# First norm of a two-layer diffusion trunk: scale weights loaded ahead of shift weights, and four query tiles taken from X times gain with the shift as a bias

## What is computed

```python
sh1, sc1, g1, sh2, sc2, g2 = silu(cond) @ ada_w[l] + ada_b[l]      # six vectors of 1024, for c_ctx and for c
h = rms_norm(x, norm1_g[l]) * (1.0 + sc1) + sh1
qa, fa_f, fa_b, ia, ga, qb, kb, vb, ob, gates = split_cols(h @ w_in, EVEN_SPLITS)
qa = silu(qa)                                                       # HGRN2 queries, 4 heads of 128
f  = lb + (1.0 - lb) * sigmoid(f_raw)                               # forget gates, per direction
```

## Time and profile before

| | us |
|---|---|
| median of three runs | 1123.31 |
| the profiled run, whole | 1123.68 |
| its span, first to last instruction | 1121.9 |
| PE busy | 1066.8 (95%) |
| DVE, ACT, POOL busy | 499.0, 412.2, 553.3 |
| mean granted PE clock | 0.981 |

### The profile page before, as it was taken

One profiled execution on the slowest core, in us unless ns is written; L12 is line 12 of the kernel. 1 busy time (PEld: TensorE's weight loads), 2 busy tenths in 40 slices (PEclk: granted clock), 3 DMA queues, 4 the chain that ended last, 5 costly groups with the idle time before them and its releaser, 6 DMA issues.

```text
span 1121.9 us, 16346 instructions
## 1 busy us (share of the span) xinstructions
PE 1066.8 (95%) x6680; PEld 974.1 (87%) x6680; DVE 499.0 (44%) x953; ACT 412.2 (37%) x687; POOL 553.3 (49%) x422
## 2 busy tenths in 40 slices
PE   4799999998999999999999998799899999999997
PEld 2598899886998999999999897765799999999997
DVE  3657888248644222222344134188473323322122
ACT  0531323356433333333223243377343333333221
POOL 0364538541536555555567343203255665665662
PEclk9799999999999999999999999889999999999999
DMA  8633444456647666655666832502034544534441
GB/s 322 220 115 116 143 171 151 149 175 242 201 130 216 188 188 188 188 176 169 191 207 198 213 114 61 141 1 76 6 108 128 135 113 118 142 94 130 122 129 57
DMA packets 202054, 166.40 MB, mean 148 GB/s; under 512 B 20269, under 2 KB 184188, under 8 KB 201852
## 3 DMA queue, kind: packets, MB, share of 16 engines
q1 hardware_dynamic: 189568, 136.79, 40.9%
q10 hardware_dynamic: 12412, 28.58, 7.4%
HBM read 162.43 MB, written 2.92 MB: 147 GB/s over the span
## 4 chain that ended last, share of the span: by engine, by line
PE 82%; DVE 6%; DMA 4%; ACT 3%; POOL 3%; issue 1%; SPq 1%; ACTq 0%; DVEq 0%
PE banks L469 21%; PE banks L471 21%; PE banks L470 21%; PE banks L563 3%; POOL w_lo L1158 2%; PE banks L540 2%; PE banks L542 2%; PE banks L541 2%; PE banks L716 2%; DMA raw<-in_ada_w 2%; PE banks L1020 1%; DVE xg_lo L1717 1%; PE banks L1036 1%; ACT w_hi L1182 1%; PE banks L556 1%
## 5 line engine op out<-in xcount | busy, mean ns | idle before, releaser
L1158 POOL TENSOR_TENSOR w_lo<-raw,w_hi 128x512 fp32r<-128x512 f32 (+2 forms) x398 | 528.0, 1356 | 551.3 <-ACT w_hi L1182 551.3
L1182 ACT ACTIVATE w_hi<-raw 128x2048 fp32r<-128x2048 f32 (+3 forms) x112 | 187.8, 1677 | 236.5 <-PE banks L471 145.3
L469 PE MATMUL banks<-xg_hi,w_hi 128*128 128x386 f32 x752 | 259.4, 345 | 0.2
L471 PE MATMUL banks<-xg_hi,w_lo 128*128 128x386 f32 x752 | 255.0, 339 | 0.0
L470 PE MATMUL banks<-xg_lo,w_hi 128*128 128x386 f32 x752 | 254.5, 338 | 0.0
L469 PE MATMUL banks<-h_hi,w_hi 128*128 128x384 f32 (+1 forms) x424 | 146.2, 345 | 6.0 <-DVE h_lo L1689 3.2
L469 PEld LDWEIGHTS banks<-xg_hi,w_hi 128*128 128x128 f32 x752 | 142.2, 189 | 7.9 <-issue 5.7
L471 PE MATMUL banks<-h_hi,w_lo 128*128 128x384 f32 (+1 forms) x424 | 142.8, 337 | 0.0
L470 PE MATMUL banks<-h_lo,w_hi 128*128 128x384 f32 (+1 forms) x424 | 142.8, 337 | 0.0
L470 PEld LDWEIGHTS banks<-xg_lo,w_hi 128*128 128x128 f32 x752 | 142.0, 189 | 0.5
L471 PEld LDWEIGHTS banks<-xg_hi,w_lo 128*128 128x128 f32 x752 | 142.4, 189 | 0.0
(11 more groups left out here) (343 smaller groups left out, 1488.6 us busy)
## 6 DMA issues: line engine op xcount, KB each, us to landing
raw<-in_ffn_w SPq DMA_DIRECT2D x88, 512.0 KB, 5.1
raw<-in_ada_w SPq DMA_DIRECT2D x28, 1024.0 KB, 6.0
raw<-in_ffn_w SPq DMA_DIRECT2D x32, 704.0 KB, 4.6
vada_raw<-in_ada_w ACTq DMA_DIRECT2D x20, 1024.0 KB, 6.5
raw<-in_w_in_even SPq DMA_DIRECT2D x18, 1024.0 KB, 5.2
raw<-in_w_out_even SPq DMA_DIRECT2D x4, 1024.0 KB, 6.0
raw<-in_w_in_odd SPq DMA_DIRECT2D x3, 1024.0 KB, 5.3
raw<-in_w_in_odd SPq DMA_DIRECT2D x8, 256.0 KB, 4.7
```

Of the source, the lines that this page charges most:

```text
L469: pe.matmul(out, s_hi, m_hi, start=first and j == 0, stop=False)
L471: mm = pe.matmul(out, s_lo, m_hi, start=False, stop=last and j == len(terms) - 1)
L1158: ins = pool.tensor_tensor(low_part(s)[:, at:to], raw[u % RAW][:, at:to], high(s)[:, at:to].bitcast(F32), ALU.subtract)
L1182: act.activation(high(s)[:, 0:n], raw[u % RAW][:, 0:n], ACT.Copy)\
```

## The change

SP loads x first, then the four scale units, then `in0` 0; the shift's four units go to buffers of their own (`shift0` to `shift3`), the first before `in0` 1 and the other three before `in0` 2. ACT squares the token-major x with a row sum; DVE puts the sums on a diagonal, and one matmul with ones spreads them. The query tiles 0 to 3 are now products of the weights with `xg = X * gain` alone (`xg_hi` by ACT, `xg_lo` by DVE), which need neither rstd nor shift. DVE multiplies their result by rstd (`take_q`). The shift's strips run after tiles 0 and 1. `shift_rows` multiplies the raw weights of `in0` 0 and 1 with the shift; the result is turned, summed and added as the bias of the Silu of the queries, which ACT does on `q` in SBUF after `first_norm`. Tiles 4 to 11 use h as before. `in0` 2 is split into `x_hi` and `x_lo`; the loads of `in0` 3 and 4 wait for `shift_rows`. The computation of the HGRN bounds moves ahead on DVE.

```diff
-SEAM_UNITS = (("up0", 0), ("in1", 3), ("up1", 0))
+SEAM_UNITS = (("in0", 2), ("up0", 0), ("in1", 3), ("up1", 0))
...
-    ada("start", 0, 6)
-    add("in0", 1, DT, 256)
-    ada("start", 6)
-    add("in0", 5, DT, 256, 1)
+    ada("start", 4)
+    add("in0", 6, DT, 256)
...
+            def start_scale(i):
+                u = number[("ada0", 4 + i)]
+                pe.wait_ge(raw_in[u % RAW], raw_need[u])
...
+            def start_shift(i):
+                pe.wait_ge(S[f"shift_in{i}"], 16)
...
+            def shift_rows(i):
+                u = number[("in0", i)]
+                w = raw[u % RAW][:, 0:2048].rearrange("p (k n) -> p k n", k=DT)
+                out = adas.fill(pe, ("in0_shift", i))
+                for k in range(DT):
+                    g = k % 4
+                    mm = pe.matmul(out[32 * g:32 * g + 32, 0:2 * P], shift[:, k, :], w[:, k, :], start=k < 4, stop=k >= 4,
+                                   skip_group_check=True)
+                mm.then_inc(adas.done, 1)
+                release[u] = (adas.done, adas.at[("in0_shift", i)] + 1)
...
+            turn_x(0, 3)
+            start_scale(0)
+            turn_x(3, 6)
+            start_scale(1)
...
-            modulation("start", 2, 6)
-            stat(0)
-            modulation("start", 6)
-            columns_to(2)
+            start_scale(2)
+            out = misc.fill(pe, ("stat", 0))
+            pe.wait_ge(S["diag_ready"], 1)
+            pe.matmul(out[:, 0:T], ones, diag[:].rearrange("p c t -> p (c t)"), start=True, stop=True).then_inc(misc.done, 1)
+            turn_x(6, 2 * NCH)
+            start_scale(3)
+            columns(("ada", 1), ("mod", 1), 1)
...
-            first_features([("in0", 0), ("in0", 1)], number[("in0", 0)], 0)
-            for j in range(2, 12):
+            first_features([("in0", 0), ("in0", 1)], number[("in0", 0)], 0, x=(xg_hi, xg_lo), signal="xg0_ready")
+            for i in range(4):
+                start_shift(i)
+            features(("in0", 2), *in0(2 * P), x=(xg_hi, xg_lo))
+            columns(("ada", 0), ("mod", 0), 0)
+            features(("in0", 3), *in0(3 * P), x=(xg_hi, xg_lo))
+            columns_made[0] = 2
+            pe.wait_ge(S["shift_ready"], 1)
+            for i in range(2):
+                shift_rows(i)
+            first_features([("in0", 4), ("in0", 5)], number[("in0", 2)], 0)
+            for i in range(2):
+                columns(("in0_shift", i), ("in0_bias", i), i)
+            for j in range(6, 12):
                 features(("in0", j), *in0(j * P))
...
+            sp.dma_start(xtok[:, 0, :], I["x_prompt"][0]).then_inc(S["x_in"], 16)
+            shifts_before = {number[("in0", 1)]: (0, 1), number[("in0", 2)]: (1, 4)}
...
-                    if native[last]:
+                    if native[last] or units[last][:2] in (("in0", 0), ("in0", 1)):
                         sp.wait_ge(*release[last])
...
+            def first_gained():
+                act.wait_ge(S["gain0"], 1)
+                for m in range(DT):
+                    for c, a, b in ((1, 0, TC), (0, TC, T)):
+                        ins = act.activation(xg_hi[:, m, a:b], X[:, m, a:b], ACT.Copy, scale=gain[:, 0, m, c:c + 1])
+                    ins.then_inc(S["xg0_hi"], 1)
...
             for c in range(NCH):
+                e = act.activation(junk[:, :], xtok[:, c, :], ACT.Square, accum_out=sumsq[:, c:c + 1])
...
+            root(0, rstd[:, 0, :])
             act.wait_ge(S["bounds_ready"], 1)
             act.activation(bound_exp[:, 0:2, :], bound_exp[:, 0:2, :], ACT.Exp).then_inc(S["bounds_exp"], 1)
+            split_to(1)
+            first_gained()
+            split_to(3)
+            first_norm()
...
+            split_to(4)
+            act.wait_ge(S["q_bias_ready"], 2)
+            for h in range(H):
+                for c, a, b in ((1, 0, TC), (0, TC, T)):
+                    e = act.activation(q[:, h, a:b], q[:, h, a:b], ACT.Silu, bias=q_bias[:, h, c:c + 1])
+                e.then_inc(S["q_ready"], 1)
+            for j in range(4, 12):
...
+                    if m == 3:
+                        take_q(2)
...
-            for m in range(DT):
-                add_squares(0, m)
+            for c in range(NCH):
+                ins = dve.tensor_scalar(diag[:, c, :], ident, sumsq[:, c:c + 1], None, ALU.mult)
...
+            gains(0)
+            dve.engine_nop().then_inc(S["gain0"], 1)
+            for m in range(DT):
+                dve.wait_ge(S["xg0_hi"], m + 1)
+                for c, a, b in ((1, 0, TC), (0, TC, T)):
+                    ins = dve.scalar_tensor_tensor(xg_lo[:, m, a:b], X[:, m, a:b], gain[:, 0, m, c:c + 1],
+                                                   xg_hi[:, m, a:b].bitcast(F32), ALU.mult, ALU.subtract)
+                ins.then_inc(S["xg0_ready"], 1)
+            dve.wait_ge(S["rstd_ready"], 1)
+            for j in range(2):
+                take_q(j)
...
+            first_norm()
+            take_q(3)
+            for i in range(2):
+                bk = adas.filled(dve, ("in0_shift", i))
...
+                dve.tensor_copy(ada_row[:, i, :], bk[:, 0:256]).then_inc(adas.read(("in0_shift", i)), 1)
+            for i in range(2):
+                bk = adas.filled(dve, ("in0_bias", i))
+                dve.tensor_reduce(q_bias[:, 2 * i:2 * i + 2, :],
+                                  bk[:, 0:256].rearrange("p (j g w) -> p j w g", j=2, g=4)[:, :, 0:2, :], AX.X, ALU.add)
...
+                dve.engine_nop().then_inc(S["q_bias_ready"], 1)
```

138 lines of the change are left out of this document (86 added, 52 removed).

## The result

The changed kernel takes 1116.37 us (median of 4 runs, 1114.49 to 1118.33), the kernel before 1124.03 in the same comparison (4 runs, 1122.07 to 1124.77). The ratio is 0.9928, interval 0.9904 to 0.9953: faster by 7.7 us. The forecast was 1119.5, a gain of 3.8. The direction holds, but the gain is twice as large as forecast. The time is inside the range of 1116.0 to 1122.8 by 0.4 us, and that is luck: the range went down so far for rival A, whose mechanism did not happen. The profiled run of the changed kernel took 1118.33 us, its span is 1116.5 us, 5.4 less than the 1121.9 of before, so the trace shows somewhat less than the median does.

A forecast was written before the change was run, and what follows sets the result against it. PE bounds the kernel and loads set its start: tile 6 could start 5.5 us earlier, less 0.8, 0.6 and 0.3 gives 3.8, so 1119.5 us. Own range 1117.5 to 1121; 8-in-10 range 1116.0 to 1122.8.

The forecast's parts named there:

- rival A: Early `xg_lo` columns are not slowed by POOL; tile 1 ends 1.9 us earlier, result 1117.3 to 1115.5; chance 0.17.
- Loads: Kernel start: with 5.5 MB instead of 9.5 ahead, `in0` 0 lands at 23.4 us, at 2.75 us per further MB.
- xg_lo beside POOL: Tiles 0 and 1: pairs take 2.1 us beside POOL; PE starts at 28.4, tiles end at 39.9, 11.8 us earlier.
- rival E: Every DVE instruction waits for a whole POOL piece; tile 1 ends at 43.8, time 1123.4, no change; chance 0.06.
- The shift's work inside the projection: After tiles 0 to 3: strips 4.2 us, product with raw weights 2.1; tile 6 could start at 64.05, 5.5 us earlier.
- What is late next: Tiles 6, 7 and 8 lose 0.8, 0.6 and 0.3 us to late splits and query bias, leaving 3.8 of 5.5.
- Behind tile 11: DVE's PF and SI work arrives later relative to tile 11; charged 0, with 3 us as upper end.
- no new PE wait after it: Sign of being right: tile 11 ends near 91 us and PE has no new wait behind it.
- B: Start 12 us earlier, but DVE or ACT falls behind by 2 to 4 us more; 1121.3 to 1123; chance 0.20.
- C: Late query bias holds ACT's queue ahead of all PF evacuations; slower than before, 1124 to 1126; chance 0.07.
- D: SP's releases or the stat chain set the start, which moves less; 1121 to 1122.5; chance 0.07.

The follow-up runs named there:

- pool_memset: Changed kernel, but POOL writes zeros as the low weight parts of the first two units instead of subtracting: 1124.93 us (one run), before 1124.9.
- second comparison: Both kernels run again without edits: the kernel before 1124.35 us, the changed kernel 1115.46 us, ratio 0.9929.
- the combinations: Changed kernel with later `in0` 1 split, shift strip 0 and nine idle matmuls ahead of tile 0: 1114.58 us; with shift work also reordered: 1114.91 us.

## Why the prediction was half right

**Loads.** Forecast: `in0` 0 landed at 23.4 us, `w_hi` at 25.3, first product at 28.4. Measured: ACT's copy starts at 23.06, ends at 24.97, first product 28.01. Right to 0.4 us, and the price per MB held up when it was tested (2.96 against 2.75 us). One figure beside it is wrong and enters no sum: before the change 7.5 MB stood ahead of `in0` 0 (six units and x), not 9.5, which is what stood ahead of PE's start besides `in0` 0 itself.

**xg_lo beside POOL.** Right in kind: 12.94 us with POOL's subtraction, 5.58 without. The forecast's choice, 2.1 us for each pair beside POOL, gave the end of tile 1 at 39.9; the strips behind it start at 40.38. PE waits twice in between, 0.36 and 0.56 us. The Trainium skill's page "SBUF — State Buffer", section "Who interferes with whom", by which rival E had 43.8, names the right pair of engines; the measured price is that of the rows of norm 1, not that of a whole POOL piece for each DVE instruction. Rival A is out: the early columns are slowed. The measured 1116.37 lies in its price of 1117.3 to 1115.5 all the same, by the gain behind tile 11. Where its mechanism was put in by hand (`pool_memset`), nothing of it arrived at tile 11.

**The shift's work inside the projection.** Strips 3.66 us where 4.2 was taken, the product with the raw weights 1.93 where 2.1 was taken, tile 6 starts at 63.84 where 64.05 was forecast. Each of them is within 0.6 us, and their sum within 0.2.

**What is late next.** Forecast: 0.8 + 0.6 + 0.3 us lost at tiles 6, 7 and 8. Tile 6 does wait for pieces of `w_lo`: its k-steps at 65.00, 66.26 and 67.52 us, two apart, start late. The starts of tile 6 in before, then of tiles 7, 8 and 9 in the changed kernel:

```profile
69.98 0.33 PE L469 MATMUL banks<-h_hi,w_hi 128*128 128x384 f32 x1
...
68.85 0.44 PE L474 MATMUL banks<-h_hi,w_hi 128*128 128x384 f32 x1
...
73.11 0.33 PE L474 MATMUL banks<-h_hi,w_hi 128*128 128x384 f32 x1
...
77.80 0.33 PE L474 MATMUL banks<-h_hi,w_hi 128*128 128x384 f32 x1
```

A tile that nothing holds up takes 4.16 us (24.96 for the six from 69.98 to 94.94 in before). Up to the start of tile 7, 0.85 us are lost where 0.8 + 0.6 were forecast, in tile 7 0.10 and in tile 8 0.53: 1.5 in all, not 1.7. ACT read tile 4 sooner than forecast, since the Silus took 2.88 us instead of 3.2, and the bias came at 64.0 (63.63 + 0.39) instead of 64.6. The larger error is in the reading of before: the forecast put its tile 6 at 69.6, by an average over ten tiles of which the first, tile 2, is slower (4.80 us, with the last pieces of `w_lo`); it starts at 69.98. So tile 6 moved by 6.14 us where 5.5 was forecast, and 6.14 - 1.48 = 4.66 at the first half row where 3.8 was forecast: an error of size, of 0.4 by the average, 0.2 by the start of tile 6 and 0.2 by the losses.

**Behind tile 11.** This is the step that failed. The forecast named only waits that the change itself could cause ("no new PE wait after it") and carried the head's gain to the end unchanged. It took for granted that the rest of the kernel is stiff: x us earlier in, x us earlier out. The runs show that it isn't. Between 187 and 742 us the same work takes 549.8 to 557.2 us, and the difference is PE's idle and its time at a granted clock of 0.50; the kernel before, with 555.5 and 554.6, is among those that pay most, the changed one has 553.2 and 551.8. What decides it stays open; the code of the change does not. Of the measured 7.7 us (8.0 in the second comparison), 4.7 are the head and some 3 this. The form of the sum was wrong more than its terms, and a gain that arises behind the head was not among the rivals at all.

**The rivals B, C and D.** Nothing was handed back inside the projection (B), the bias was in time (C), the start was where it was put (D). DVE, though, is busy for 41.0 of 44 us from 52 to 96 us, 10 us more than before, and the combinations show that this is the room that is now used up: B is what happens to the next change here.
